# First mixer: query products placed between the transposes, query norm finished inside the attention

## What is computed

```python
q  = (rms_norm(c_q, g_qa) @ w_qb).reshape(b, s, 16, 192)
kv = (rms_norm(c_kv, g_kva) @ w_kvb).reshape(b, s, 16, 128 + 128)
k_nope, v = split(kv)                       # k = [k_nope, shared k_rope]
q, k = rms_norm(q, g_q), rms_norm(k, g_k)   # per head
q, k = rotate the last 64 columns of each by cos, sin
o = softmax(q @ k.T / sqrt(192), chunk-causal mask) @ v
return o.reshape(b, s, 16 * 128) @ w_o
```

## Time and profile before

| | |
|---|---|
| median of 3 runs | 3583.55 us (3583.06 to 3585.41) |
| the profiled execution | 3579.43 us |
| its span, first to last instruction | 3577.5 us |
| PE busy | 2869.6 us (80%) |
| DVE busy | 2037.9 us (57%) |
| ACT busy | 946.3 us (26%) |
| POOL busy | 1422.9 us (40%) |
| mean granted TensorE clock | 0.917 of full speed |

### The profile page before, as it was taken

One profiled execution on the slowest core, in us unless ns is written; L12 is line 12 of the kernel. 1 busy time (PEld: TensorE's weight loads), 2 busy tenths in 40 slices (PEclk: granted clock), 3 DMA queues, 4 the chain that ended last, 5 costly groups with the idle time before them and its releaser, 6 DMA issues.

```text
span 3577.5 us, 26686 instructions
## 1 busy us (share of the span) xinstructions
PE 2869.6 (80%) x7322; PEld 1347.5 (38%) x7322; DVE 2037.9 (57%) x3580; ACT 946.3 (26%) x2345; POOL 1422.9 (40%) x1065
## 2 busy tenths in 40 slices
PE   7888967777777888888878788998987877777776
PEld 6445743333332333333333333443433322222222
DVE  2334156666767554555554665455555466777765
ACT  3334322222222222323221222232322122222221
POOL 4002645565665322222432432322333255555553
PEclk8877989998998999999999899999999998888888
DMA  4212599999999999999999999999999999999998
GB/s 145 83 62 81 194 384 416 416 414 417 416 417 422 418 417 417 417 417 418 416 419 417 413 417 417 417 417 417 416 400 419 417 408 418 418 417 420 415 417 357
DMA packets 246468, 1345.34 MB, mean 376 GB/s; under 512 B 27200, under 2 KB 48192, under 8 KB 113984
## 3 DMA queue, kind: packets, MB, share of 16 engines
q0 software_dynamic: 147456, 1073.81, 72.5%
q1 hardware_dynamic: 98880, 269.99, 19.8%
HBM read 1341.62 MB, written 2.10 MB: 376 GB/s over the span
## 4 chain that ended last, share of the span: by engine, by line
DMA 64%; PE 20%; issue 11%; DVE 3%; POOL 1%; ACT 1%; SPq 1%; DVEq 0%; POOLq 0%; ACTq 0%
DMA room<-in_peer_v_dram,index 64%; PE psum L982 12%; PE psum L1033 3%; PE psum L745 1%; PE psum L746 1%; PE psum L747 1%; POOL room L673 1%; DVE room L1962 0%; DVE resid L1973 0%; POOL room L683 0%; DMA room<-in_peer_u_dram,index 0%; SPq L544 0%; POOL w_low L657 0%; SPq L514 0%; PE psum L948 0%
## 5 line engine op out<-in xcount | busy, mean ns | idle before, releaser
L982 PE MATMUL psum<-room,diag 128*128 128x512 f32 x3072 | 1636.2, 675 | 628.1 <-DMA room<-in_peer_v_dram,index 581.6
L1962 DVE CUSTOM_DVE_ANT_0 room<-room,normed 128x2048 f32<-128x2048 f32 x512 | 1172.9, 2291 | 664.4 <-DMA room<-in_peer_u_dram,index 660.0
L982 PEld LDWEIGHTS psum<-room,diag 128*128 128x128 f32 x3072 | 607.2, 210 | 1595.4 <-issue 1257.2
L683 POOL DMA_INDIRECT room<-in_peer_v_dram,index x512 | 748.5, 1462 | 1070.2 <-PE psum L982 1039.9
L673 POOL DMA_INDIRECT room<-in_peer_u_dram,index x512 | 558.3, 1090 | 757.9 <-DVE dots L1962 529.6
L1033 PE MATMUL psum<-wbuf,normedT 128*128 128x512 f32 x1536 | 695.1, 595 | 0.0
L1392 ACT ACTIVATE acts<-dots 128x1 f32<-128x1 f32 x512 | 103.6, 202 | 1832.2 <-DVE dots L1962 1831.8
L1973 DVE SCALAR_TENSOR_TENSOR resid<-room,acts,resid 128x512 f32<-128x512 f32 x512 | 384.4, 751 | 290.9 <-DMA room<-in_peer_v_dram,index 289.1
L1033 PEld LDWEIGHTS psum<-wbuf,normedT 128*128 128x128 f32 x1536 | 285.3, 191 | 330.7 <-issue 327.6
L657 POOL TENSOR_TENSOR w_low<-wbuf,w_high 128x2048 fp32r<-128x2048 f32 (+1 forms) x28 | 113.9, 4076 | 305.1 <-ACT w_high L1247 305.1
L1401 ACT ACTIVATE diag<-ident,acts 128x128 f32<-128x128 f32 x512 | 205.5, 401 | 48.3 <-ACT acts L1396 1.5
(11 more groups left out here) (197 smaller groups left out, 1742.8 us busy)
## 6 DMA issues: line engine op xcount, KB each, us to landing
wbuf<-in_fox_w_in_dram SPq DMA_DIRECT2D x128, 1024.0 KB
wbuf<-in_fox_w_o_dram SPq DMA_DIRECT2D x32, 1024.0 KB
wbuf<-in_peer_w_q_dram SPq DMA_DIRECT2D x32, 1024.0 KB
wbuf<-in_mla_w_o_dram SPq DMA_DIRECT2D x16, 1024.0 KB, 5.2
wbuf<-in_peer_w_q_dram SPq DMA_DIRECT2D x32, 512.0 KB, 8.9
wbuf<-in_mla_w_in_dram SPq DMA_DIRECT2D x8, 1024.0 KB, 8.2
wbuf<-in_mla_w_kvb_dram SPq DMA_DIRECT2D x32, 256.0 KB, 3.5
room<-in_peer_u_dram,index POOLq DMA_INDIRECT x512
```

Source lines behind the costliest of these rows:

```text
L683: pool.indirect_dma_start(v_ring[:, r, :], None, v_table, bass.IndirectOffsetOnAxis(index[:, number % 2, s:s + 1], 0)).then_inc(v_full[r], 16)
L982: mm = pe.matmul(psum[:, q, :], diag[:, r, :], v_ring[:, r, q * TILE:(q + 1) * TILE], start=at == 0, stop=at == WINDOW - 1, skip_group_che ...
L1962: V.tensor_tensor_reduce(u_ring[:, r, :], u_ring[:, r, :], normed[:, b, :], 1.0, 0.0, ALU.mult, ALU.add, dots[:, r:r + 1]).then_inc(dot_do ...
```

## The change

In the program of PE, the pieces of the q products of group g+1 move ahead of the attention of group g: three between the transposes of q and of k of group g, the fourth behind those of k. The kv pieces then stand behind attention steps 0 to 3, and steps 4 to 6 have none. The two halves of `wbuf` are released separately: kv's of group g behind the third q piece, q's of group g+1 behind step 0.

On ACT, the copy of q for g+1 moves from step 4 to the place ahead of the attention; its root moves from behind the attention into step 4; and the root of k moves from the end of the loop's body into the next turn, between the copies of q's and of k's transposes. On DVE, the squares of q move from step 4 to step 2, and the rest of q's norm from behind the attention into step 5, which is the last step there, so it keeps its place in the order of DVE.

```diff
-COPY_Q_AT = 4
+SQUARES_AT = 2
+ROOTS_AT = 4
+NORM_AT = 5
...
-                run(mla_products(0))
+                run(mla_products(0, 0))
+                kv = mla_products(0, 1)
+                run(kv[0:2])
+                release(0, 0)
+                run(kv[2:4])
                 with pe.Fori(0, mla.groups - 1) as g:
-                    for kind in range(2):
-                        qk_transposes(mla, g, kind)
-
-                    steps, pieces = attention(mla, g), mla_products(g + 1)
-                    for i in range(max(len(steps), len(pieces))):
-                        run(steps[i:i + 1])
-                        run(pieces[i:i + 1])
+                    ahead = mla_products(g + 1, 0)
+                    qk_transposes(mla, g, 0)
+                    run(ahead[0:3])
+
+                    release(g, 1)
+                    qk_transposes(mla, g, 1)
+                    run(ahead[3:4])
+
+                    steps, kv = attention(mla, g), mla_products(g + 1, 1)
+                    for i, step in enumerate(steps):
+                        step()
+                        if i == 0:
+                            release(g + 1, 0)
+                        run(kv[i:i + 1])
                 for kind in range(2):
                     qk_transposes(mla, mla.groups - 1, kind)
+                release(mla.groups - 1, 1)
                 run(attention(mla, mla.groups - 1))
...
                 def copy_kv(g):
-                    roots(mla, g, 0)
...
-                    roots(mla, g, 1)
-
-                def both_transposed(g):
-                    for kind in range(2):
-                        transposed(mla, g, kind)
+
+                def both_transposed(g):
+                    transposed(mla, g, 0)
+                    roots(mla, g, 1)
+                    transposed(mla, g, 1)
 
                 copy_q(0)
+                roots(mla, 0, 0)
                 copy_kv(0)
                 with act.Fori(0, mla.groups - 1) as g:
                     both_transposed(g)
-                    attention(mla, g, lambda step: step == COPY_Q_AT and copy_q(g + 1))
+                    copy_q(g + 1)
+                    attention(mla, g, lambda step: step == ROOTS_AT and roots(mla, g + 1, 0))
                     copy_kv(g + 1)
...
-                        attention(at, g, lambda s: s == COPY_Q_AT and head_norms(at, g + 1, 0, part=0))
-                        head_norms(at, g + 1, 0, part=1)
+                        def query_norm(s):
+                            if s == SQUARES_AT:
+                                head_norms(at, g + 1, 0, part=0)
+                            if s == NORM_AT:
+                                head_norms(at, g + 1, 0, part=1)
+
+                        attention(at, g, query_norm)
                     head_norms(at, g + 1, 1)
```

More of the change, by code:

```diff
@@ L862, in run, with mla_products, piece @@
                     step()
[L864 to L868, removed]
+            def mla_products(g, t):
+                (wh, wn), (gh, gn) = mla.w(g, t), mla.g(g, t)
+                n = (2 * MLA_QK, 2 * (NOPE + VDIM))[t]
+                def piece(b, ks):
                     if ks[0] == 0:
@@ L877, in piece, with release @@
                         last.then_inc(g_full[gh], 1)
[L878 to L886, removed]
+                return [lambda b=b, ks=ks: piece(b, ks)
+                        for b in range(NB) for ks in (range(0, RC // 2), range(RC // 2, RC))]
+            def release(g, t):
+                (wh, wn), (gh, gn) = mla.w(g, t), mla.g(g, t)
+                pe.wait_ge(g_full[gh], 2 * gn + 2)
+                pe.sem_inc(w_used[wh], 1)
             def mla_groups():
```

## The result

The changed kernel takes 3563.37 us (median of 8 runs, 3556.06 to 3571.92), the kernel before 3583.31 (8 runs, 3578.13 to 3586.81): ratio 0.9946, 95% interval 0.9933 to 0.9958, 19.9 us less. The forecast was 12.9 us less, 3570.6, with 3560 to 3580 as its range. The profiled execution took 3562.60 us, with a span of 3560.6.

A forecast was written before the change was run, and what follows sets the result against it. Bound by PE's chain and TensorE's clock: periods of 25.9 + 2.0 = 27.9 us against 30.7 bring the last group 13.6 us earlier; less 0.7 for output weights, net 12.9, giving 3570.6 us, range 3560 to 3580.

The forecast's parts named there:

- What sets a group: In the first mixer, a chain of work on PE and TensorE's clock, 2.4 or 1.2 GHz, set each group's time.
- Step 4: In the attention, four kv pieces widen by 0.43 us each, so step 4 begins at 12.48 us instead of 10.76.
- PE is never waiting there: Ahead of attention step 4, PE has no waits, so four pieces wider by 0.43 us each count in full.
- Period at full clock: From one group's logits until PE is free for the next: 25.9 us without any low clock.
- Clock: On PE, the clock falls and rises 4.0 us after the q products start; half is lost, 2.0 us per group.
- Group 0: Its logits come at 118.2 instead of 115.31, behind added products and transposes: a loss of 2.9 us.
- Last period: The period to the last group's logits has no products ahead: 15.2, 6.7 and 1.9 make 23.8 us.
- Load of the output weights: Requested 1.5 us ahead of the last logits instead of 6.5; 0 to 2 us lost, taken as 0.7.
- kv's weights: Requested at about 19.6, landed at 25.0, needed at 26.7 or later: hidden, with 1.7 us to spare.
- the price of the placement: On PE, three q products between the transposes hold k's transposes up by 1.9 us.
- the table load: On ACT before q's root: 1.28 us without a drain; the skill's rule would cost 9.7 us over seven periods.

The follow-up runs named there:

- the filled kernels: Four kernels with unread matmuls in PE's idle stretches, which take the clock out: ratios 0.9896, 0.9913, 0.9866 and 0.9944.
- the filled kernel: The changed kernel with unread matmuls added in PE's idle stretches: 3547.99 us, ratio 0.9896 to the kernel before.
- the last experiment: The changed kernel with kv's half of the weight buffer released ahead of the last group's transposes instead of behind them: 3559.62 us in one run.
- the filled kernel before: The kernel before, root and order unchanged, with unread matmuls in PE's idle stretches: 3552.86 us, ratio 0.9913.
- the changed order and the late root: The changed kernel with q's root behind the attention again: ratio 0.9974; with unread matmuls in PE's idle stretches too, 0.9944.
- filled with the early root alone: The kernel before with q's root in step 5 and unread matmuls in PE's idle stretches: 3536.52 us, ratio 0.9866.

## Why the prediction was right, point by point

- **What sets a group** (chain on PE, and the clock): right, shown by the filled kernels.
- **Step 4** was forecast at 12.48 us behind the first logits, and stands at 184.58 - 172.46 = 12.12. The last division ends at 14.17 (forecast 14.35), the reciprocal starts at 14.86 (15.2), the q products at 19.48 (19.9). Each is a little early: the wider pieces do cost PE 1.7 us, but "PE is never waiting there" was wrong by 0.2 us. Behind the table load for exp it waited 0.18 us in group 0 of the kernel before, and under the wider pieces it does not.
- **Period at full clock**: forecast 25.9; 25.0 in the filled kernel, which goes without q's transposes at half clock. The term was 0.9 too large, of which 0.4 was there when the q products start.
- **Clock**: forecast 2.0 per group; 27.35 - 25.0 = 2.4. The rise came 4.3 us after the start of the products (191.94 to 196.28), forecast 4.0. (The shortest of the three in the earlier trace rows is 3.8 and not 4.0: a clock of 0.93 in the row of 145.50 puts the rise at 145.57.) The two terms are off in opposite directions, 0.9 and 0.4, so that their sum is better than its parts. Together the period was forecast at 27.9 and came to (281.98 - 116.93) / 6 = 27.5: 2.3 us over six groups.
- **Group 0**: the stretch from its first transposes to its logits is 6.5 us (110.45 to 116.93) against 3.9, so 2.5 lost, forecast 2.9. It also began 0.9 us earlier (110.45 against 111.37), and 0.7 of that comes from the change: before, the releases stand behind the last kv piece, and PE waits there until its products are complete ([0.50 <-PE psum L874] in the earlier trace rows); in the changed kernel that release stands behind the third q piece, and the transposes follow the products at once, 12.13 us after the first product instead of 12.79. The forecast had put this at nothing.
- **Last period**: 23.7, forecast 23.8.
- **Load of the output weights**: forecast 0.7 lost, measured 1.3, and by the last experiment it is this load. The mistake was to think of the last quarter; the first three were late, by 2.9 us on ACT in all.
- **kv's weights**: requested at 191.81, ahead of the first of the three pieces; no wait. PE's sequencer runs ahead, as taken.

Up to the output projection this makes 16.0 us (342.29 to 326.26), and 16.9 us of span in the profiled executions. The forecast was 12.9 for both; the periods are the largest part of the difference, 2.3 us. The median of the runs moved by 19.9. The other 3.0 us are explained by no term: the runs of the changed kernel spread over 16 us and those before over 9, and one profiled execution of each says no more than that. Two of the filled kernels spread by less than 2 us (3547.35 to 3549.06; 3535.96 to 3537.63), so the moment at which the clock falls and rises in an execution may make the spread. But the filled kernel before spreads over 4.4 us in four runs without a fall up to the last group, and the changed kernel with all q pieces behind k's transposes over only 6.1 in eleven, with a fall in every turn. Where the spread comes from is open.

What the prediction did not see is the weight of the two halves. It walked the changed order with the changed root and summed both. It named the price of the placement, k's transposes held up by 1.9 us (3.6 in the trace, half of it at half clock), but set against it only the old order with the old root. That the old order hides q's norm under products, once its root is early, was in the earlier trace rows: products run to 193.03 there and DVE idles beside them until 191.62.

On the table load, the time behind it in the changed kernel:

```profile
185.49 0.28 ACT L1347 ACTIVATE share<-psum 128x128 f32 x1
...
187.08 0.21 ACT L1227 ACTIVATE stat<-stat 128x4 f32<-128x4 f32 x1
```

The copy ahead of the load ends at 185.77, the load runs from 185.79 to 187.07, and the root starts at 187.08. The rule of the Trainium skill (ScalarE: Activation LUTs, What ACT_TABLE_LOAD costs), 2.66 us for a switch, does not hold in this kernel: from the end of the copy to the root it is 1.31 us.

## What to carry to other kernels

When a change moves work into a gap, ask first what made the gap: here it was a table load and a root queued behind work that did not need them, and moving that one instruction pair alone gave 29 us, more than moving it together with the matmuls. Where TensorE idles once per loop turn, price the turn at full clock and the clock apart (here 25.7 and 5.0 us of 30.7); matmuls that nobody reads are a cheap probe for it, and here, with the early root in the old order, also gave the fastest kernel (3536.5 us, ratio 0.9866, interval 0.9850 to 0.9883). Test the halves of a change against the old kernel as well as against the new one.

## What the hardware showed beyond that

The clock can rise on transposes alone. In the trace of the kernel before, at the start of the mixer, the timeline has:

```profile
94.05 3.84 PE L707 MATMUL psum<-ident,room 128*128 128x128 f32 x16 [2.82 <-DVE room L1722]
...
98.58 0.59 PE L874 MATMUL psum<-wbuf,room 128*128 128x384 f32 x1 [0.69 <-ACT room L1279]
```

and the view of stretches has the rise here:

```profile
97.50:98.00 0.50, 0.39 (x2) 0.00 (x0) 0.47 (x4) 0.24 (x2) 0.00 (x0) 0.72 1.01 381
```

The clock was low before these 16 fp32 transposes and rose at about 97.8 us, ahead of the first product. PE had been idle for 2.8 us ahead of them. The Trainium skill (TensorE: Matmul & The Clock Gate, Part 4: PE-mode transpose) says that transposes do not count as work for the clock in the way matmuls do, and that full clock does not engage for them; here the clock rose on a dense row of them. It did so in eight of the ten profiled kernels; in the two others (all q pieces behind k's transposes; filled with the early root alone) it rose at 99.8 and 98.9 us, 4.5 and 3.4 us into the products. And two to four unread matmuls of 0.86 us each a turn kept the clock at 1.00 up to the last group in three kernels, through stretches of 5 to 7 us in which PE had no products, where without them it fell in nearly every turn; with the changed order and the late root, whose idle stretch is the longest, three were not always enough.

A subtraction on DVE, 1.2 us long by itself (before, from 348.74, with POOL done), took up to 5.6 us beside POOL's subtractions of 4.5 us each. It ended 1.1 us behind the POOL instruction that was running when it began: in the kernel before POOL's runs from 336.58 to 341.11, DVE's from 339.29 to 342.19; with the changed order and the late root both start at 331.98, POOL's ends at 336.50 and DVE's at 337.59. In the changed kernel DVE's began at 324.94, 0.08 us ahead of POOL's next, and took 1.22 us, and POOL's took 5.57 instead of 4.5. So these instructions went one after the other, whichever came first, and a few tenths of a microsecond decide about 4.4. That one engine holds up the other is read from these times; no run took POOL's work away.
